# A hybrid attention and expert block on one core: four key rows of the first unit moved ahead of its value rows, five more query-weight pieces loaded ahead of the rows

## What is computed

```python
def peer_ffn(xn, wq, keys1, keys2, U, V):          # xn: 256 x 2048
    q = (xc @ wq).reshape(B, C, 8, 256)            # 8 heads
    s1 = einsum('bchd,nd->bchn', q[..., :128], keys1)
    s2 = einsum('bchd,nd->bchn', q[..., 128:], keys2)
    v1, i1 = top_k(s1, 16); v2, i2 = top_k(s2, 16)
    sc, ci = top_k((v1[..., :, None] + v2[..., None, :]).reshape(..., 256), 16)
    e = take(i1, ci // 16) * 128 + take(i2, ci % 16)
    g = softmax(sc)
    a = gelu(einsum('bchkd,bcd->bchk', U[e], xc))  # 16 rows of U per token and head
    return einsum('bchk,bchkd->bcd', g * a, V[e])  # the same 16 rows of V
```

## Time and profile before

| | before |
|---|---|
| median of three runs | 2161.99 us (2160.67 to 2166.12) |
| the profiled execution | 2166.0 us, of which the span is 2164.3 us |
| TensorE matmul busy | 1870.4 us, 86% |
| VectorE busy | 1291.3 us, 60% |
| ScalarE busy | 581.4 us, 27% |
| GpSimd busy | 708.8 us, 33% |
| DMA moved | 699.85 MB, mean 323 GB/s |
| granted TensorE clock | 0.997 of full speed |
| chain that ended last | TensorE 54%, DMA 38% |

### The profile page before, as it was taken

How to read it: one execution, slowest core, us unless ns; L and a number is a source line. 1 busy time by engine, 2 the same in 40 slices (tenths; PEclk the granted TensorE clock), 3 DMA queues, 4 the chain that set the end, 5 groups by cost and what they waited for, 6 DMA issues and landing times.

```text
span 2164.3 us, 22175 instructions
## 1 busy us (share of the span) xinstructions
PE 1870.4 (86%) x6551; PEld 1108.9 (51%) x6551; DVE 1291.3 (60%) x2180; ACT 581.4 (27%) x1060; POOL 708.8 (33%) x624
## 2 busy tenths in 40 slices
PE   9999999999999999999977777777777777777777
PEld 7888887878888886544332232222222222222222
DVE  5544557787866556776356456556556556546444
ACT  5544445555544442211111111111111111111101
POOL 2000010110000001554455445445455555545542
PEclk9999999999999999999999999999999999999999
DMA  7666753444457577999999999999999999999997
GB/s 264 190 185 200 222 152 114 136 117 121 134 173 238 190 242 264 415 404 415 421 422 421 421 421 422 422 422 422 422 422 422 423 422 422 422 422 422 422 421 325
DMA packets 163011, 699.85 MB, mean 323 GB/s; under 512 B 15569, under 2 KB 23793, under 8 KB 96657
## 3 DMA queue, kind: packets, MB, share of 16 engines
q0 software_dynamic: 74176, 537.35, 59.8%
q1 hardware_dynamic: 88784, 161.89, 23.9%
q10 hardware_dynamic: 2, 0.01, 0.0%
HBM read 697.10 MB, written 2.10 MB: 323 GB/s over the span
## 4 chain that ended last, share of the span: by engine, by line
PE 54%; DMA 38%; issue 4%; DVE 1%; POOL 1%; ACT 0%; POOLq 0%; DVEq 0%; ACTq 0%
DMA v_ring<-in_peer_v_dram,idx_v 32%; PE banks L1223 10%; PE banks L758 10%; PE banks L760 10%; PE banks L759 10%; DMA big<-in_peer_u_dram,idx_u 6%; PE banks L1192 4%; PE banks L880 2%; PE banks L736 1%; PE banks L1116 1%; DVE big L2299 1%; PE banks L864 1%; PE banks L871 1%; POOL v_ring L620 1%; PE banks L1163 1%
## 5 line engine op out<-in xcount | busy, mean ns | idle before, releaser
L1223 PE MATMUL banks<-v_ring,kxT 128*128 128x512 f32 x1920 | 884.3, 604 | 268.4 <-DMA v_ring<-in_peer_v_dram,idx_v 267.3
L2299 DVE SCALAR_TENSOR_TENSOR big<-big,xn 128x2048 f32<-128x2048 f32 x256 | 586.7, 2292 | 417.2 <-DMA big<-in_peer_u_dram,idx_u 409.3
L1223 PEld LDWEIGHTS banks<-v_ring,kxT 128*128 128x128 f32 x1920 | 347.6, 190 | 802.5 <-ACT kxT L1688 394.6
L611 POOL DMA_INDIRECT big<-in_peer_u_dram,idx_u x256 | 354.1, 1383 | 217.0 <-DVE big L2299 120.2
L620 POOL DMA_INDIRECT v_ring<-in_peer_v_dram,idx_v x240 | 281.8, 1174 | 410.8 <-PE banks L1223 365.6
L1784 DVE TENSOR_TENSOR ws<-wraw,ws 128x1024 fp32r<-128x1024 f32 (+1 forms) x248 | 294.8, 1195 | 187.9 <-ACT ws L1342 185.8
L1688 ACT ACTIVATE kxT<-ident,ga 128x128 f32<-128x128 f32 x240 | 95.4, 401 | 957.1 <-PE banks L1223 952.5
L1342 ACT ACTIVATE ws<-wraw 128x1024 fp32r<-128x1024 f32 (+1 forms) x248 | 254.4, 1032 | 219.1 <-PE banks L760 202.3
L758 PE MATMUL banks<-ws,xr 128*128 128x512 f32 x736 | 294.2, 400 | 0.9 <-DVE h L2075 0.9
L760 PE MATMUL banks<-ws,xr 128*128 128x512 f32 x736 | 287.4, 390 | 0.0
L759 PE MATMUL banks<-ws,xr 128*128 128x512 f32 x736 | 286.8, 390 | 0.0
(11 more groups left out here) (308 smaller groups left out, 1463.7 us busy)
## 6 DMA issues: line engine op xcount, KB each, us to landing
wraw<-in_w_in_dram SPq DMA_DIRECT2D x152, 512.0 KB, 3.6
wraw<-in_w_out_dram SPq DMA_DIRECT2D x32, 512.0 KB, 4.0
wraw<-in_w_xkv_dram SPq DMA_DIRECT2D x16, 512.0 KB, 6.9
wraw<-in_w_branch_da_dram SPq DMA_DIRECT2D x16, 512.0 KB, 3.8
wraw<-in_w_branch_nsa_dram SPq DMA_DIRECT2D x16, 512.0 KB, 4.1
wq<-in_peer_wq_dram SPq DMA_DIRECT2D x16, 512.0 KB, 9.9
wraw<-in_w_xq_dram SPq DMA_DIRECT2D x8, 512.0 KB, 3.7
wb<-in_peer_wq_dram SPq DMA_DIRECT2D x8, 512.0 KB, 7.0
```

Source lines behind the costliest of these rows:

```text
L611: nc.gpsimd.indirect_dma_start(u_ring[:, r, :], None, peer_u[0], bass.IndirectOffsetOnAxis(ap=idx_u[par][:, j:j + 1], axis=0)).then_inc(u_ ...
L1223: last = nc.tensor.matmul(V_BANKS[c][n], diag[:, r, :], v_ring[:, r, n * NW:(n + 1) * NW], start=(first and j == 0), stop=(final and j == ...
L2299: V.scalar_tensor_tensor(out=u_ring[:, r, :], in0=u_ring[:, r, :], scalar=1.0, in1=xn3[:, par, :], op0=ALU.mult, op1=ALU.mult, accum_out=d ...
```

## The change

- `QR` is 23 places: one is added at `later[:, 0:1024]`, where the queries of the cross-attention lie. Piece 0 goes there (`raw_slot`), and its load stands after pieces 4 to 7, behind a wait for the last score matmul of the cross-attention (`sc_ready`). The other early pieces move down by one place, so that `wb`'s last place is free for piece 14.
- Pieces 15 to 18 are loaded ahead without a wait into four places called `held`: two in chunk 1's half of `xn3`, two in chunk 1's half of `xf` (the transposed normed tokens), the latter with 512 bytes per run. ScalarE copies each to its real place (`move_held`, four copies of 128x1024) when `xo_pass` has freed that, and TensorE waits for `held_moved` in place of the landing.
- Pieces 19 to 22 now wait for `xo_done`, and pieces 23 to 31 for `wq_used`.
- `x_scratch` moves to `big[:, 3 * D:4 * D]`, which is slot 3 of `u_ring`. So U row 3 waits for the last value matmul of the cross-attention (`pv_ready`).
- VectorE's `xo_out` of chunk 1 waits for `held_moved` before it writes over `held`.
- GpSimd: U rows 12 to 15 of unit 0 are issued ahead of its V rows. Since piece 14 lies in the last quarter of `v_ring`, V row 3 is issued after `wq_used` 15 and after U row 3 of unit 1.

```diff
-QR = 22
+QR = 23
+HELD = 15
+HOLDS = 4
...
-    if g < 2 * HP:
-        return 11 + g
-    if g < 11:
-        return g
-    if g < 14:
-        return 19 + (g - 11)
-    return (0, 1, 2, 3, 4, 5, 6, 7, 19, 20)[(g - 14) % 10]
+    if g < HELD:
+        return (22, 11, 12, 13, 14, 15, 16, 17, 8, 9, 10, 19, 20, 21, 18)[g]
+    return (0, 1, 2, 3, 4, 5, 6, 7, 19, 20, 21)[(g - HELD) % 11]
...
-        x_scratch = xn3[:, 1, :]
+        x_scratch = big[:, 3 * D:4 * D]
...
+        held = [xn3[:, 1, f:f + KS * NW].rearrange("p (k j n) -> p k j n", k=KS, n=P) for f in (0, KS * NW)]
+        held += [xf[:, f:f + 8, P:2 * P].rearrange("p (k j) n -> p k j n", k=KS) for f in (0, 8)]
...
-            for g in range(HP):
+            for g in range(1, HP):
                 raw_piece(g)
...
-            for g in range(2 * HP, 14):
+            sp.wait_ge(sc_ready, 48 + X_H + LAG)
+            raw_piece(0)
+            for g in range(2 * HP, HELD):
                 raw_piece(g)
-            for g in range(14, RAWS):
-                if g < 22:
-                    sp.wait_ge(xo_done, X_H + (g - 14) // 2 + 1)
+            for m in range(HOLDS):
+                n = (HELD + m) % PIECES
+                tile = 1 + (HELD + m - 2 * HP) // PIECES
+                for k in range(KS):
+                    sp.dma_start(held[m][:, k], pq[n][:, k, tile * NW:(tile + 1) * NW].rearrange("p (j n) -> p j n", n=P)).then_inc(held_landed[m], 16)
+            for g in range(HELD + HOLDS, RAWS):
+                if g < HELD + 8:
+                    sp.wait_ge(xo_done, X_H + (g - HELD) // 2 + 1)
                 else:
-                    sp.wait_ge(wq_used, g - 10 + (g >= 24))
+                    sp.wait_ge(wq_used, g - 11 + (g >= HELD + 11))
                 raw_piece(g)
...
-            for j in range(1, RING):
+            for j in range(1, RING - 1):
                 fetch_u(0, j, 0)
+            pool.wait_ge(pv_ready, 48 + X_H + LAG)
+            fetch_u(0, RING - 1, 0)
...
+            for j in range(12, PK):
+                fetch_u(0, j, 0)
             keep_indices(0, 0)
             pool.wait_ge(wq_used, 2 * HP)
-            for j in range(RING):
+            for j in range(RING - 1):
                 fetch_v(0, j, 0)
-            for j in range(12, PK):
-                fetch_u(0, j, 0)
             pool.wait_ge(idx_ready, 2)
             keep_indices(1, 1)
             for j in range(PK):
+                if j == RING:
+                    pool.wait_ge(wq_used, HELD)
+                    fetch_v(0, RING - 1, 0)
                 fetch_u(1, j, 1)
...
+            def move_held(m):
+
+                act.wait_ge(xo_done, X_H + m // 2 + 1)
+                act.wait_ge(held_landed[m], 16 * KS)
+                A(raw_pieces[raw_slot(HELD + m)].rearrange("p k (j n) -> p k j n", n=P), held[m], ACT.Copy).then_inc(held_moved, 1)
+
+            move_held(0), move_held(1)
+            h_square(0, 1)
+            move_held(2), move_held(3)
+            h_square(1, 1), h_square(2, 1)
...
+                if c == 1:
+                    dve.wait_ge(held_moved, n // 2 + 1)
```

More of the change, by code:

```diff
@@ L108 @@
 U_LEAD = 4
-QR = 22
+QR = 23
+HELD = 15
+HOLDS = 4
 RAWS = 2 * HP + (N_PQ - 1) * PIECES
 def raw_slot(g):
-    if g < 2 * HP:
-        return 11 + g
-    if g < 11:
-        return g
-    if g < 14:
-        return 19 + (g - 11)
-    return (0, 1, 2, 3, 4, 5, 6, 7, 19, 20)[(g - 14) % 10]
+    if g < HELD:
+        return (22, 11, 12, 13, 14, 15, 16, 17, 8, 9, 10, 19, 20, 21, 18)[g]
+    return (0, 1, 2, 3, 4, 5, 6, 7, 19, 20, 21)[(g - HELD) % 11]
 def raw_turn(g):
-    return 1 if g < 14 else 2 + (g - 14) // 10
+    return 1 if g < HELD else 2 if g < HELD + 15 else 3
 EVENS = PK // 2
@@ L261, in block_program @@
         raw_pieces = [wq[:, s, :, :] for s in range(8)] + [later[:, f:f + KS * NW].rearrange("p (k n) -> p k n", k=KS) for f in (2048, 3072, 5120)] + [wb[:, s, :, :] for s in range(8)] + [product_t[:, f:f + KS * NW].rearrange("p (k n) -> p k n", k=KS) for f in (0, KS * NW)]
-        raw_pieces.append(aside[:, 0:KS * NW].rearrange("p (k n) -> p k n", k=KS))
+        raw_pieces.extend(m[:, 0:KS * NW].rearrange("p (k n) -> p k n", k=KS) for m in (aside, later))
+        held = [xn3[:, 1, f:f + KS * NW].rearrange("p (k j n) -> p k j n", k=KS, n=P) for f in (0, KS * NW)]
+        held += [xf[:, f:f + 8, P:2 * P].rearrange("p (k j) n -> p k j n", k=KS) for f in (0, 8)]
         scores = later[:, 0:UNITS * 256]
@@ L368, in block_program @@
             sem, ("dot_done", "v_used", "route_scores", "route_exp", "gelu_done", "ga_ready", "diag_ready", "vacc_free", "y_done"))
+        held_landed = [sem(f"held_landed{m}") for m in range(HOLDS)]
+        held_moved = sem("held_moved")
         wq_landed = [sem(f"wq_landed{r}") for r in range(QR)]
@@ L1184, in raw_tile_piece @@
                 g = 2 * HP + (i - 1) * PIECES + n
-                pe.wait_ge(wq_landed[raw_slot(g)], 16 * raw_turn(g))
+                if HELD <= g < HELD + HOLDS:
+                    pe.wait_ge(held_moved, g - HELD + 1)
+                else:
+                    pe.wait_ge(wq_landed[raw_slot(g)], 16 * raw_turn(g))
                 if n == 0 and i == 1:
@@ L1658, in _ @@
             ox_T(1)
-            for q in range(3):
-                h_square(q, 1)
+            def move_held(m):
[6 more added lines that the diff above has]
+            h_square(1, 1), h_square(2, 1)
             for q in range(3):
```

## The result

| | before | after |
|---|---|---|
| median, runs taken together | 2163.41 us (2160.09 to 2166.31, 8 runs) | 2170.63 us (2168.84 to 2173.57, 8 runs) |
| ratio | | 1.0033, 95% interval 1.0024 to 1.0042 |
| the profiled execution | 2166.0 us, span 2164.3 us | 2173.1 us, span 2171.4 us |

The change costs 7.2 us, 0.33%: slower, and the time is 0.6 us above the upper end of the range. I had forecast +3.0. The range of 2158 to 2170 us was laid around the median of three runs before, 2161.99 us, so as a difference it was -4 to +8 us, and +7.2 lies inside that; the median of eight runs before is 1.4 us higher, and this alone puts 2170.63 above the end. The forecast of +3.0 is wrong by 4.2 us either way.

The account below looks back on a forecast made before the run. The DMA engines' row-fetch rate was taken as the bound in the last 1300 us. -7.0 + 3.5 + 4.3 + 4.6 - 2.4 = +3.0 us on the median 2161.99 gave 2165.0 us; own range 2161 to 2169, 8-in-10 range 2158 to 2170.

Parts of the forecast that it names:

- What bounds the kernel: Last 1300 us: DMA engines' row-fetch rate bounds; the change of the total is the difference in issued work undelivered at 1020.06.
- Five pieces out: Pieces 14 to 18 leave the row phase, at 1.4 us each: -7.0 us, bounds -6.2 and -7.3.
- The four ScalarE copies: Copies after each `xo_pass`, and VectorE's wait for them: 0, upper end 0.7 us.
- Gap A: DMA engines idle from 852.9 us until U row 4's data at 856.4: about +3.5 us.
- Gap B: DMA engines idle from 881.8 us until U row 12's data at about 886.1, its slot awaiting dot 8: +4.3 us.
- Gap C: DMA engines idle from 891.1 us until piece 23's data at about 895.7, U row 14 awaiting dot 10: +4.6 us.
- What comes back: Put-off work fills the earlier shortfalls at 940 to 960 and 1000 to 1020 us: -2.4 us, between 0 and -2.5.
- GpSimd stands at the same place at 1020.06: At 1020.06 us GpSimd, in its fixed order of U and V rows, waits for TensorE at the same place.
- V rows come late to TensorE: Unit 1 starts later, V row 5 lands after 966.5 us and TensorE waits: +8 us, 2170; chance 0.15.
- only gap A: Around 880 us the queue is long enough that only the gap at 853 us opens: -3.5 us, 2158.5; chance 0.17.
- won whole: Every gap is made up before 1020 us, so the pieces' full gain stays: -7.0 us, 2155.0; chance 0.07.
- shorter lags: In each of three gaps data starts 1.2 us sooner, as the issue instruction ends: -0.6 us, 2161.4; chance 0.14.

Follow-up runs that it names:

- e2: The changed kernel with V rows 0 to 2 issued ahead of U rows 12 to 15 again, five pieces still loaded ahead; ratio 1.0002 to the kernel before.
- e1: The kernel before with only U rows 12 to 15 moved ahead of V rows 0 to 3, every piece loaded as before; 2171.56 us, ratio 1.0039.
- e5: The changed kernel with V rows 4 to 7 of unit 0 issued two U rows of unit 1 earlier; ratio 1.0022 to the kernel before.

## Why the prediction was wrong, point by point

- **What bounds the kernel: right.** That the difference is only what is undelivered when the saturated part begins is what the ledger shows, for twelve kernels.
- **Five pieces out: mis-sized, by 0.8 us.** I took 1.4 us for a piece, the ledger takes 1.24, the price at 422 GB/s. Over the eight kernels with five pieces ahead the ledger's change is 0.3 us under the measured one on average; with 1.4 it would be 1.1 under. The 360 GB/s of the earlier trace rows are those of a stretch with such loads alone.
- **The early end of the loads: right.** Near full until 833 us (368 GB/s), 2 GB/s from 835.
- **Piece 0, U row 3, the scratch: right, 0.** TensorE's head-0 matmuls start at 828.64 (before 828.83), and GpSimd's first four rows come as before.
- **The four ScalarE copies: right, 0.** ScalarE's timeline has `849.42 2.00` and `852.90 2.01` for the two pairs, and VectorE's dots start at 851.40, 855.06 and 858.72, at most 0.2 us from before.
- **Gap A +3.5: 3.3 measured. Gap B +4.3: 4.4 (883 to 893 us). Gap C +4.6: 4.2.** Together 11.9 against 12.4. Gap B's size is in part luck. I had it from 881.8 to 886.1; the engines run empty only at about 884 and nothing flows until 887.5, since the issue of U row 12 lasts 2.94 us in place of 0.94, with a dot running beside it.
- **A term that the sum lacks: 1.2 us from 873 to 883 us.** There the engines are busy (share 1.00) and move 369 GB/s in place of 421. e2, with the pieces ahead and the old order, has this too (364), and e1, with the new order alone, has 421: it comes with the early pieces. Why isn't shown.
- **"What comes back" -2.4: this step failed.** On balance nothing came back. From 903 us on the shortfall is 3.8 us before and 3.9 after: 903 to 943 and 973 to 1103 us lost less (0.7 against 2.0), 943 to 973 more (3.2 against 1.8). I had taken "the backlog that the gaps leave" for work that waits in the DMA queues. It waits on GpSimd, behind slots: the U ring's four are freed by dots, V rows 4 to 7 stand behind U rows in the fixed order, and the dots and V row 4 came 7 us later. e5 shows it from the other side: with the V rows moved in the order, the stretch fills.
- **The sum.** +3.0 became +7.1 by 0.8 (pieces), 0.7 (gaps, less 0.5, and the stretch before gap B, 1.2) and 2.5 (nothing back), with rounding. The upper end of the forecast's own range, +6.9, had the pieces at 6.2 and nothing back, which is what happened; that it comes so near is also luck, since its last 0.7 us were for VectorE held up by the copies, which cost nothing. The middle of +3.0, and with it the chance of 0.75 for "within 0.3%", hung on the one term that no row showed.
- **"GpSimd stands at the same place at 1020.06": wrong.** It is 5.1 us late there, although it was in step at V row 11 (983.94 us): in between it waits for U slots, whose dots are 7.2 us late. So the difference was already on the issuing engine, not only in the queue. This is the same error as the failed step.
- **Rival "V rows come late to TensorE": not as described.** V row 5's slot starts at 966.34 us, without a wait, so its point of decision was not met. The time came out as this rival had it (2170), by another mechanism. TensorE's first wait is at 1024, not at 1030, and 6.4 us in sum, not 3. The rival's own sum was wrong too: it took 0.8 us for the loss of what would come back, which the forecast had at 2.4, so it should have been +9.6.
- **Rivals "only gap A", "won whole", "shorter lags": excluded** by three gaps and their sizes. The Trainium skill (DMA: Bandwidth & Descriptors, Specifications) has about 1 us to the first byte of a GpSimd transfer. Here U row 12's issue starts at 883.96 and ends at 886.90, and the engines are at 0 GB/s until about 887.5: 3.5 us from its start, 0.6 from its end. The first row's issue in the kernel before runs from 840.75 to 841.84, and in windows of 0.5 us its first bytes move between 842.5 and 843.0: 1.8 to 2.3 us from the start, 0.7 to 1.2 from the end. So the page's figure agrees with this trace if it is counted from the end of the issue. Counted from the start, as the prediction did, it doesn't; it would have made the gaps 3.9 us smaller than the 12.4 forecast, and 11.9 were measured.
- **Signs:** U row 12 at 884, right; V row 0 at 898, was 901.87, since U rows 14 and 15 and the copy of the indices took 2.94, 2.10 and 1.99 us beside dots; unit 1's first dot at 915, was 920.34, behind that and the three V rows; dot 12 without a wait and earlier, right (896.50 against 899.78); a constant 2 to 5 us from 1040 us on, was 7.

**Open:** whether more U slots would let the early pieces win their 6.2 us was not tried. Nor was a kernel in which all of unit 1 comes earlier behind the same gaps. It isn't shown why the stretch before the first U row differs by up to 5.4 us between executions.

## What to carry to other kernels

In a part that the DMA engines bound, sum what they fail to move: in this kernel each such microsecond went to the end. It could only have been made up by issued work that waits for the engines, and a queue in a fixed order behind a few slots held no such reserve here; a fetch moved ahead was missing later. The eleven variants of order and early loads had 7 to 21 us of shortfall, the kernel before 6.0, and none was faster. Before putting requests that wait for a computing engine ahead of requests that could go at once, look at what else would be in the queue in that time.

## What the runs showed of the hardware that I had not expected

- **An indirect DMA's issue waits for VectorE's dot.** Alone it takes 0.94 us on GpSimd; where a dot of two SBUF inputs starts first it ends some 0.8 us after the dot. U row 12's issue runs from 883.96 to 886.90, beside the dot of 883.79 to 886.08. The copy of 128x16 indices does the same: 1.99 us, from 899.61 to 901.60, beside the dot of 899.25 to 901.54. The Trainium skill (SBUF — State Buffer, Who interferes with whom) says that a VectorE instruction with two SBUF inputs contends with a GpSimd instruction that reads SBUF; the copy agrees. The indirect DMA reads its row numbers too (`idx_u` is one of its inputs in the trace), so its 2.94 us agree as well. The same section infers that writing a DMA's descriptors is not held up by such an instruction; no run here tells the reading of the row numbers from the writing of the descriptors.
- **The issues of the loads with 512-byte runs took SyncE longer, and cost the kernel nothing.** SyncE's timeline after, the held pieces in halves:

```profile
818.57 3.85 SPq L518 DMA_DIRECT2D xn<-in_peer_wq_dram  x4
822.46 7.06 SPq L518 DMA_DIRECT2D big<-in_peer_wq_dram  x4
```

  An issue into the normed tokens takes 3.85 / 4 = 0.96 us, one into their transpose (512-byte runs) 7.06 / 4 = 1.77 us (8.20 / 4 = 2.05 in e2); both end ahead of the rows. That the length of the runs is the cause isn't shown: the loads were also issued one behind the other.
